# The front stage of a two-layer encoder: x fetched in eight pieces, a second V tile, and the latents' passes spread over the rounds

## What is computed

```python
def rmsnorm(x, g):
    xf = x.astype(jnp.float32)
    y = xf * lax.rsqrt(jnp.mean(xf * xf, axis=-1, keepdims=True) + EPS)
    return y.astype(x.dtype) * g
...
def even_mixer(h, pos, layer_idx, w_in, q_norm, w_uq, kv_norm, w_ukv,
               lq1, lk1, lq2, lk2, subln, w_out):
    b, s, _ = h.shape
    proj = h @ w_in                                             # (B,S,EVEN_IN)
    c_q, c_kv, k_rope, qkv_d = jnp.split(
        proj, [MLA_Q_RANK, MLA_Q_RANK + MLA_KV_RANK,
               MLA_Q_RANK + MLA_KV_RANK + MLA_ROPE_DIM], axis=-1)
...
    q = (rmsnorm(c_q, q_norm) @ w_uq).reshape(b, s, MLA_HEADS, MLA_NOPE_DIM + MLA_ROPE_DIM)
    kv = (rmsnorm(c_kv, kv_norm) @ w_ukv).reshape(b, s, MLA_HEADS, MLA_NOPE_DIM + MLA_V_DIM)
...
    q = jnp.concatenate([q[..., :MLA_NOPE_DIM], apply_rope(q[..., MLA_NOPE_DIM:], cos, sin)], axis=-1)
    k_r = apply_rope(k_rope, cos, sin)                          # (B,S,rope) shared by all heads
...
    h = x
    for i in range(DEPTH):
...
            h = h + even_mixer(rmsnorm(h, e_attn_norm[j]), pos, i, e_w_in[j], e_q_norm[j],
...
            h = h + odd_mixer(rmsnorm(h, o_attn_norm[j]), row, col, o_w_qkv[j],
                              o_q_norm[j], o_k_norm[j], o_w_out[j])
        h = h + swiglu(rmsnorm(h, ffn_norm[i]), w_gate[i], w_up[i], w_down[i])
    return rmsnorm(h, final_norm)
```

## Time and profile before

| | us |
|---|---|
| runs shown | 6479.17, 6088.32, 6100.59 |
| their median | 6100.59 |
| profiled execution | 6115.31 |
| its span on the slowest core (core 5) | 6113.8 |
| spans of the eight cores | 6054.7 to 6113.8 |
| front stage, up to its last matmul | about 311 |
| first S matmul of the attention stage | 325.81 |

### The profile page before, as it was taken

One profiled execution on the slowest core, in us unless ns is written; L12 is line 12 of the kernel. 1 busy time (PEld: TensorE's weight loads), 2 busy tenths in 40 slices (PEclk: granted clock), 3 DMA queues, 4 the chain that ended last, 5 costly groups with the idle time before them and its releaser, 6 DMA issues. The chain is left out here.

```text
span 6113.8 us, 98370 instructions; the slowest of 8 cores (6054.7 to 6113.8 us)
## 1 busy us (share of the span) xinstructions
PE 5728.7 (94%) x28568; PEld 2416.5 (40%) x28568; DVE 2922.8 (48%) x4008; ACT 4128.2 (68%) x6667; POOL 1056.8 (17%) x1104
## 2 busy tenths in 40 slices
PE   5789999998999999999999989799999999999998
PEld 1234444442334334444434434334344444444443
DVE  4633333333555555555555555445444444445443
ACT  3479899997776767676767663386766666666641
POOL 2323224310112121322221324300000000000000
PEclk8899999999999999999999999899999999999999
DMA  5557647504334334444334335312222322223234
GB/s 145 146 153 225 173 136 225 170 19 104 77 106 121 113 112 137 114 136 123 127 113 133 110 134 153 112 58 75 70 93 93 105 92 93 96 90 107 87 105 144
DMA packets 314097, 722.57 MB, mean 118 GB/s; under 512 B 41072, under 2 KB 101744, under 8 KB 307952
## 3 DMA queue, kind: packets, MB, share of 16 engines
q1 hardware_dynamic: 304112, 689.72, 37.2%
q0 software_dynamic: 9472, 26.55, 1.7%
HBM read 596.40 MB, written 125.30 MB: 118 GB/s over the span
## 5 line engine op out<-in xcount | busy, mean ns | idle before, releaser
L203 ACT ACTIVATE P<-S 128x512 bf16<-128x512 f32 (+1 forms) x5120 | 3277.0, 689 | 1150.4 <-PE S L197 1083.3
L197 PE MATMUL S<-Qt,Kt 128*128 128x512 bf16 (+1 forms) x6144 | 2176.2, 381 | 90.6 <-ACT P L203 31.2
L197 PE MATMUL O<-P,Vt 128*128 128x512 bf16 x6144 | 2171.6, 380 | 6.7 <-DVE os L223 4.8
L197 PE MATMUL F<-hn,wgu 128*128 128x512 bf16 x5456 | 1418.6, 380 | 33.4 <-DMA wgu<-gu 18.1
L197 PEld LDWEIGHTS S<-Qt,Kt 128*128 128x128 bf16 (+1 forms) x6144 | 597.2, 98 | 1085.7 <-issue 564.3
L197 PEld LDWEIGHTS O<-P,Vt 128*128 128x128 bf16 x6144 | 600.1, 98 | 661.6 <-issue 28.8
L197 PEld LDWEIGHTS F<-hn,wgu 128*128 128x128 bf16 x5456 | 532.4, 98 | 670.4 <-issue 53.4
L197 PE MATMUL F<-ac,wdn 128*128 128x512 bf16 x2618 | 673.4, 379 | 8.7 <-DMA wdn<-dn 4.4
L226 DVE RECIPROCAL rc<-lc 32x128 f32<-32x128 f32 x512 | 480.8, 939 | 43.5 <-DVE rc L226 2.3
L208 DVE TENSOR_TENSOR hb<-hb,F 128x512 f32<-128x512 f32 x256 | 175.7, 686 | 586.9 <-PE F L197 582.0
L232 POOL DMA_DIRECT2D outT<-of x64 | 34.6, 541 | 2119.9 <-DVE of L211 2035.5
(11 more groups left out here) (130 smaller groups left out, 4593.5 us busy)
## 6 DMA issues: line engine op xcount, KB each, us to landing
wgu<-gu SPq DMA_DIRECT2D x341, 512.0 KB, 3.4
wf<-w_gu SPq DMA_DIRECT2D x44, 1024.0 KB, 9.7
wdn<-dn SPq DMA_DIRECT2D x64, 704.0 KB, 4.3
wdn<-dn SPq DMA_DIRECT2D x110, 352.0 KB, 3.3
Kt<-kd SPq DMA_DIRECT2D x128, 256.0 KB, 6.6
Vt<-vd SPq DMA_DIRECT2D x128, 256.0 KB, 6.4
gu<-wb SPq DMA_DIRECT2D x44, 512.0 KB, 6.2
wf<-w_dn SPq DMA_DIRECT2D x32, 704.0 KB, 7.4
```

Of the source, the lines that this page charges most:

```text
L197: self.S.op("tensor", lambda e: e.matmul(out, lhsT=lhsT, rhs=rhs, start=start, stop=stop), reads, writes)
L203: self.S.op("scalar", lambda e: e.activation(out=out, in_=in_, func=func, scale=scale), reads, writes)
```

## The change

x is requested in eight pieces of one chunk each, with a semaphore for each, one piece every second step of a round, as a fourth generator `load_x(j+3)`. `norm` writes one chunk of hn a step instead of two, and its last squares stand in the same step as its ssq matmuls. `latents` runs four matmuls a step over six steps, in PSUM banks of its own (`lat`, three); heads have four banks and ssq one. There are two `vt` tiles. In the attention stage `lv` is loaded through POOL's queue, and a head's pieces are requested as K, Q, V of the first quarter, K and V of the others, and the rest of Q last.

```diff
--- before.py
+++ after.py
@@ -373,7 +373,7 @@
     Wl = kb.sb(st, "Wl", [128, 8, 384], BF16)
     Wuq = kb.sb(st, "Wuq", [128, 2, 2, 768], BF16)
     Wkv = kb.sb(st, "Wkv", [128, 1024], BF16)
-    hbs = Rot([kb.sb(st, "hb", [128, 8, T], F32, 2) for _ in range(2)])
+    hbs = Rot([kb.sb(st, "hb", [128, 8, T], F32, 8) for _ in range(2)])
     tms = [kb.sb(st, "tm", [96, 2, T], F32) for _ in range(3)]
     sqs = Rot([kb.sb(st, "sq", [128, T], BF16) for _ in range(8)])
     lqs = Rot([kb.sb(st, "lq", [128, T], BF16) for _ in range(3)])
@@ -385,18 +385,20 @@
     kos = Rot([kb.sb(st, "ko", [128, T], BF16) for _ in range(3)])
     cqs = [[kb.sb(st, "cq", [128, T], BF16) for _ in range(2)] for _ in range(2)]
     cks = [kb.sb(st, "ck", [128, T], BF16) for _ in range(2)]
-    vts = Rot([kb.sb(st, "vt", [128, 8, 4, 128], BF16) for _ in range(1)])
-    pps = Rot([kb.ps(st, "pp", [128, 512]) for _ in range(6)])
-    ssqs = Rot([kb.ps(st, "ssq", [128, 512]) for _ in range(2)])
+    vts = Rot([kb.sb(st, "vt", [128, 8, 4, 128], BF16) for _ in range(2)])
+    pps = Rot([kb.ps(st, "pp", [128, 512]) for _ in range(4)])
+    P = [kb.ps(st, "lat", [128, 512]) for _ in range(3)]
+    ssqs = Rot([kb.ps(st, "ssq", [128, 512]) for _ in range(1)])
     vmv = vm.rearrange("h p (j c) -> p h j c", c=128)
     wv = Wkv.t[:].rearrange("p (h c) -> p h c", c=128)[:, :, 64:128]
 
     def load_x(j):
-        hb = hbs.next()
-        for p in range(2):
-            c = slice(p * 4, p * 4 + 4)
-            kb.dma("sync", hb.t[:, c, :], xv[:, c, j * T:(j + 1) * T], (), [hb.cb[p]], hb.cb[p])
-        return hb
+
+        hb = xs[j]
+        for c in range(8):
+            kb.dma("sync", hb.t[:, c, :], xv[:, c, j * T:(j + 1) * T], (), [hb.cb[c]], hb.cb[c])
+            yield
+            yield
 
     def load_tab(j):
         tm = tms[j % 3]
@@ -416,8 +418,8 @@
     def norm(j, hb):
         sq = []
         for c in range(8):
-            sq.append(squares(sqs, hb.t[:, c, :], 128, [hb.cb[c // 4]]))
-            if c % 2:
+            sq.append(squares(sqs, hb.t[:, c, :], 128, [hb.cb[c]]))
+            if c % 2 and c < 7:
                 yield
         ssq = ssqs.next()
         for c in range(8):
@@ -426,21 +428,23 @@
         yield
         hn = hnA[j]
         for c in range(8):
-            kb.stt(hn.t[:, c, :], hb.t[:, c, :], gn.t[:, c:c + 1], rs.t[:], ALU.mult, ALU.mult, [hb.cb[c // 4], gn.b, rs.b], [hn.b])
-            if c % 2:
-                yield
+            kb.stt(hn.t[:, c, :], hb.t[:, c, :], gn.t[:, c:c + 1], rs.t[:], ALU.mult, ALU.mult, [hb.cb[c], gn.b, rs.b], [hn.b])
+            yield
 
     def latents(j):
         hn, tm = hnA[j], tms[j % 3]
         t0 = j * T
         cq, ck = cqs[j % 2], cks[j % 2]
-        P = [pps.next() for _ in range(3)]
-        for p in range(3):
+        sq = []
+        for p, rows in ((0, 128), (1, 64), (2, 128)):
             for k in range(8):
                 kb.mm(P[p].t[:], Wl.t[:, k, p * 128:(p + 1) * 128], hn.t[:, k, :], k == 0, k == 7, [Wl.b, hn.b], [P[p].b])
-        s0 = squares(lqs, P[0].t[:], 128, [P[0].b])
-        s1 = squares(lqs, P[1].t[0:64, :], 64, [P[1].b])
-        s2 = squares(lqs, P[2].t[:], 128, [P[2].b])
+                if k == 3:
+                    yield
+            sq.append(squares(lqs, P[p].t[0:rows, :], rows, [P[p].b]))
+            if p < 2:
+                yield
+        s0, s1, s2 = sq
         t1, t2, ob = t1s.next(), t2s.next(), obs.next()
         kb.tt("vector", t1.t[0:32, :], P[1].t[64:96, :], tm.t[64:96, 0, :], ALU.mult, [P[1].b, tm.b], [t1.b])
         kb.tt("vector", t2.t[0:32, :], P[1].t[96:128, :], tm.t[64:96, 1, :], ALU.mult, [P[1].b, tm.b], [t2.b])
@@ -490,7 +494,8 @@
         while gens:
             gens = [g for g in gens if next(g, 0) is None]
 
-    x = load_x(0)
+    xs = [hbs.next() for _ in range(NB)]
+    run(load_x(0))
     kb.dma("gpsimd", Wl.t[:], w_lat.rearrange("p (k c) -> p k c", k=8), (), [Wl.b], Wl.b)
     kb.dma("gpsimd", Wuq.t[:], w_uq2.rearrange("p (v k c) -> p v k c", v=2, k=2), (), [Wuq.b], Wuq.b)
     kb.dma("gpsimd", Wkv.t[:], w_ukv, (), [Wkv.b], Wkv.b)
@@ -498,17 +503,14 @@
         kb.memset("vector", v.t[:, :, :, 64:128], 1.0, [v.b])
     for cq in cqs:
         kb.memset("vector", cq[1].t[64:128, :], 0.0, [cq[1].b])
-    xs = [x, load_x(1)]
     load_tab(0)
+    run(load_x(1))
     load_tab(1)
     run(norm(0, xs[0]))
-    xs.append(load_x(2))
-    run(norm(1, xs[1]), latents(0))
+    run(norm(1, xs[1]), latents(0), load_x(2))
     for j in range(NB):
         if j + 2 < NB:
             load_tab(j + 2)
-        if j + 3 < NB:
-            xs.append(load_x(j + 3))
         if 2 <= j < 6:
             kb.dma("gpsimd", Wd.t[:, 2 * j - 4:2 * j - 2, :], w_dif[j - 2].rearrange("p (k c) -> p k c", k=2), (), [Wd.b], Wd.b, fill=True)
         work = [heads(j)]
@@ -516,6 +518,8 @@
             work.append(latents(j + 1))
         if j + 2 < NB:
             work.append(norm(j + 2, xs[j + 2]))
+        if j + 3 < NB:
+            work.append(load_x(j + 3))
         run(*work)
 
 def stage_c(kb, st, ones, gn, Kt, Vt, qg, kg, vg, h2v, ov, gu16, dn16, oo16):
@@ -1251,7 +1255,7 @@
                     loaded.append((dst, w, wf))
 
             lam_init = 0.8 - 0.6 * math.exp(-0.3 * 0)
-            kb.dma("sync", lv.t[:], lamv, (), [lv.b], lv.b)
+            kb.dma("gpsimd", lv.t[:], lamv, (), [lv.b], lv.b)
             kb.tt("vector", ltmp.t[:, 0, :], lv.t[:, 0, :], lv.t[:, 1, :], ALU.mult, [lv.b], [ltmp.b])
             kb.tt("vector", ltmp.t[:, 1, :], lv.t[:, 2, :], lv.t[:, 3, :], ALU.mult, [lv.b], [ltmp.b])
             S.op("vector", lambda e: e.reduce_sum(out=lsum.t[:, 0:1], in_=ltmp.t[:, 0, :], axis=AX.X), [ltmp.b], [lsum.b])
@@ -1269,9 +1273,13 @@
                     h = idx
                     for p in range(4):
                         c = slice(p * 1024, p * 1024 + 1024)
+                        kb.dma("sync", Kt.t[0:96, c], km[h][:, c], (), [Kt.cb[p]], Kt.cb[p])
+                        if p == 0:
+                            kb.dma("sync", Qt.t[0:96, c], qm[h][:, c], (), [Qt.cb[p]], Qt.cb[p])
+                        kb.dma("sync", Vt.t[:, p * 8:p * 8 + 8, :], vm[h][:, c].rearrange("p (j c) -> p j c", c=128), (), [Vt.cb[p]], Vt.cb[p])
+                    for p in range(1, 4):
+                        c = slice(p * 1024, p * 1024 + 1024)
                         kb.dma("sync", Qt.t[0:96, c], qm[h][:, c], (), [Qt.cb[p]], Qt.cb[p])
-                        kb.dma("sync", Kt.t[0:96, c], km[h][:, c], (), [Kt.cb[p]], Kt.cb[p])
-                        kb.dma("sync", Vt.t[:, p * 8:p * 8 + 8, :], vm[h][:, c].rearrange("p (j c) -> p j c", c=128), (), [Vt.cb[p]], Vt.cb[p])
 
             heads = [load_head_tiles(i) for i in range(8)]
             jobs = []
```

## The result

| | before | changed |
|---|---|---|
| median of the runs, us | 6491.32 | 6212.85 |
| lowest and highest | 6081.33 to 6987.04 | 6065.78 to 6973.89 |
| first S matmul, mean of the eight cores | 322.1 | 309.4 |
| first S matmul, last core | 325.8 | 316.2 |

This ratio is 0.9968, 95% interval [0.9954, 0.9983]. **The change saves about 20 us (10 to 28) of some 6095**, no change at the level of 2%. I had forecast 38.

A forecast was written before the change was run, and what follows sets the result against it. Only the front stage, 5% of the span, could change, with DVE's work and waits setting its rounds. 28.5 + 9.9 + 0 + 0.4 = 38.8, called 38 us, gave 6077 us for the profiled execution, 6063 from the median; range 6034 to 6094.

The forecast's parts named there:

- The bound on the class: Whole kernel: front stage is 5% of the span, so over 2% (122 us) needs more than a third of it gone.
- the signs: Profile after: lq waits gone, cq under 1 us, gap 4 to 6 us at q2's t, first S at 288 us.
- the first rival: Front stage rounds: the last x piece lands late beside Wd, 15 us lost at 9.1 us a piece; chance 0.16.
- The start: Start of the front stage: 1.6 us saved on ACT's squares, later waits against it; about 0, within 2 either way.
- too few banks: Heads in all eight rounds: DVE waits for PE at every head, 83 to 122 us lost, about 6160; chance 0.07.
- six rounds, 28.5 us saved: Six full rounds: 21.5 us DVE work plus 8.8 idle makes 30.3 us a round, 182 us in all.
- 5 us: hidden: Last x piece of a round: taken to land in 5 us with 6 us available, so no wait.
- last two rounds, 9.9 us saved: Rounds 6 and 7: 17.8 us instead of 23.92 and 11.9 instead of 15.67; bounds 6 and 12.
- hand-over, 0.4 saved, at worst 1 lost: Front stage to first S: K, Q, V issued first, lv off SP, 0.4 us earlier; lv by POOL may lose 1.
- Sum: Whole kernel: 28.5 + 9.9 + 0 + 0.4 = 38.8, called 38 us saved.

The follow-up runs named there:

- e1: Changed kernel with the 768 KB Wd load of rounds 2 to 5 asked for in mid-round; 6048.84 us against 6092.51 before, first S at 289.2.
- e12: Changed kernel with Wd in mid-round, the norm's ssq a step later and lv by SP; 6078.71 us against 6101 to 6109 before.
- e14: Changed kernel with Wd in mid-round and lv by SP; ratio 0.9928 to the kernel before, 6046.10 to 6054.97 us.
- e4: Changed kernel with one V tile instead of two; 6102.66 us, first S at 341.3.
- e3: Changed kernel with x asked for as before, two 1 MB pieces at the round's start; 6087.73 us, first S at 314.3.

## Why the prediction was wrong

**What held.** The bound on the class: the front stage is 5% and nothing behind it moved. DVE's own work of 21.5 us a round (192.6 us less 64.8 of waits is 21.3 a round). Of the signs: no lq waits, cq waits 1.1 us at most, no vm waits, one large gap a round at q2's t, and the small km writes in 3.56 us. The gap itself was 8.21 us where I had written 4 to 6, the first S came at 309 and not at 288, and ACT waited for x, the sign that I had given for the first rival. For the km writes, SP's row of round 2, core 2, answers to the earlier trace rows:

```profile
134.20 3.56 SPq L232 DMA_DIRECT2D km<-ob  x8
```

Rounds 0 and 1 took 29.5 and 28.1 us against 30.3 forecast. The start came out 1.7 us earlier, inside its ±2. Against "too few banks", DVE's t waits four times in round 2 of e1, 6.9 us in all, of which 4.49 at one place, and not at each of eight heads.

**Step "six rounds, 28.5 us saved".** Measured 14.6 (core 2, 207.2 to 192.6). What failed is the choice "5 us: hidden". The price of the piece was taken "near the short writes since the burst is gone" although I had the load of `Wd` in four rounds in the rival's "For". The slack was 5.4 us, not 6 (asked for at 118.00, ACT ready at 123.43), and the piece took 8.4 there and up to 10.0 in the other three; away from `Wd` it took 3.5 to 4.9, as I had it. Without the late piece (e1) the saving is 28.3, but that it meets the 28.5 so closely is in part luck: rounds 0 to 2 are 1 to 3 us shorter than the 30.3 forecast, and rounds 3 to 5 up to 2.4 longer, with 17.4 us of ko waits that I had taken as gone. So the first rival is what happened, at a chance of 0.16; its price of 9.1 us a piece was nearly right, its loss of 15 us is 14 here. It struck in the four rounds with `Wd`, not in five.

**Step "last two rounds, 9.9 us saved".** Measured -1.6 (39.8 to 41.4). I counted the vt wait as removed and "most" of the ko waits. Here the wait does stand behind the V write: without the vt wait ACT runs on to the three ko tiles and waits there 4.61 us, up to 281.89, 6.9 us behind SP's request of the write of V (275.03). I had worked DVE's rate, 1.43 us a head, as if ACT never stood. Round 6 took 20.6 us (17.8 forecast), round 7 18.8 and its tail (11.9). Even with five ko tiles the two take 37.1 us, where 29.9 (39.8 - 9.9) would follow from the forecast. DVE then waits for PE in them 8.6 us; whether for want of banks or for the lower clock (0.82 in round 7) was not tested and stays open.

**Step "hand-over, 0.4 saved, at worst 1 lost".** On core 2 the first S stands 11.7 us behind the last V write before and after; over the eight cores it is 12.2 us before and 11.5 after, so the order of the loads and lv's leaving SP brought 0.7 at most. lv by POOL cost more than my bound. Before, core 2, ACT's exponential of the sums and its first P:

```profile
319.17 0.20 ACT L203 ACTIVATE lsum<-lsum 128x2 f32<-128x2 f32 x1
...
320.30 1.94 ACT L203 ACTIVATE P<-S 128x1024 bf16<-128x1024 f32 x2 [0.92 <-PE S L197]
```

That is 1.1 us behind S at 319.19; after, P starts 3.0 us behind S (304.50 to 307.51), and with lv on SP again 1.1 (e12; e14's core 1: 292.69 to 293.80). So the first P loses 1.9 us: I set the load's 4.8 us against 2.45 us of free time and left out that the table load (1.28 us at 306.11) stands behind it on ACT as well. Whether these 1.9 us reach the end of the kernel is not shown; what follows the first S is no longer than before (5747 against 5749 us).

**Sum, core 2, up to the first P:** 1.7 + 14.6 - 1.6 - 1.9 = 12.8 us where 38 stood; the ratio says 20 (10 to 28). The second V tile, whose gain I took as included in the rounds, was the part without which nothing would have been gained (e4: S 341.3).

## What to carry to other kernels

A small load that an engine waits for in order has to be priced with the largest transfer that is asked for at the same moment, also from another queue; where slack and landing are within a microsecond or so of each other, move the large one first, and look at what it stands beside in its new place: here most of the waits for small writes then stood beside it. A wait removed for one tile is a gain only if the next tile that is written on the same way has room: price them together, and buy depth for the small, frequent one. The worth of a buffer is not the sum of its waits before: it was 2 us, within the scatter, in the old order and 32 in the new. And before a run is aimed at a wait, look at which transfer was asked for just ahead of it: two of these runs were aimed at the write of V, and most of the waits stood beside `Wd`.

## What the runs showed of the hardware

- A 256 KB piece of x took 8.4 to 10.0 us to land where a load of 768 KB had been asked for 0.8 to 0.9 us ahead of it on another queue, and 3.5 to 4.9 us at the same place without that load (changed kernel and e1, core 2, four rounds each), with a 1 MB write asked for 1.0 to 2.4 us behind it in both; over the first 400 us the two had these medians (changed kernel, core 2, DMA issues: count, KB each, us to landing), with V's write and lv:

```profile
hb<-xT SPq DMA_DIRECT2D x64, 256.0 KB, 5.7
vm<-vt SPq DMA_DIRECT2D x8, 1024.0 KB, 10.4
...
Wd<-w_dif POOLq DMA_DIRECT2D x4, 768.0 KB, 8.8
...
lv<-lamv POOLq DMA_DIRECT2D x1, 128.0 KB, 5.1
```

- lv took 5.1 us by POOL's queue and 3.1 by SP's (changed kernel and e14, core 2; 2.7 on core 5 before). By SP it was asked for ahead of the head's first load, by POOL 0.5 us behind it, so queue and place are not separated.
- The V write in two halves, whose rows in HBM are half as long (512 bytes), went with longer ko waits, 33.8 us against 23.5. Moving the whole write to another queue left them as they were (22.9). Why the halves cost more was not separated from their coming at two moments.
- The Trainium skill, page "DMA: Bandwidth & Descriptors", section Bandwidth, would have transfers batched to a megabyte or more. Here the eight pieces of 256 KB were 5 to 8 us better in S than two of 1 MB (e3): ACT waited 5.3 us for small writes instead of 39.3, and 13.3 for x instead of 0. The DMA engines were 0.63 busy in the full rounds. The trace does not bear the rule out as a guide to the stage's time; of the rate of a single transfer, which the rule is about, no run here says anything against it.
- A granted clock of 0.84 instead of 0.88 in round 2 went with a DVE gap of 8.21 us instead of 4.49, and 0.75 with the last full round; the rounds' PE time was 144.32 us against 139.50 in e1. How much of the 20 us is the clock and how much the wait was not separated.
